# First two column tiles of the recurrent layer's input: turned by VectorE from PSUM and carried by DMAs, in place of ScalarE staging and TensorE transposes

## The reference

```python
WIDTH = 1536          # 12 chunks of 128 channels
def recurrent_mixer(h, w_in, conv_w, conv_b, gate_w, gate_b, lam, w_out):
    u = jnp.einsum('bsd,dc->bsc', h, w_in)
    gate, xb = u[..., :WIDTH], u[..., WIDTH:]
    xb = causal_depthwise_conv(xb, conv_w, conv_b)      # 4 taps along the tokens
    y = rg_lru(xb, gate_w, gate_b, lam)
    return jnp.einsum('bsc,cd->bsd', y * jax.nn.silu(gate), w_out)
# rg_lru: per chunk of 128 channels g = sigmoid(u @ gate_w + gate_b), split in r and i,
#   log_a = -8 * r * softplus(-lam); h_t = a_t * h_(t-1) + sqrt(1 - a_t^2) * (i * u)_t
```

## Time and profile before

| what | value |
|---|---|
| median of three executions | 880.54 us |
| the profiled execution | 880.93 us |
| its span, first to last instruction | 879.2 us |
| TensorE (PE) busy | 870.7 us, 99% of the span |
| VectorE (DVE) busy | 594.1 us, 68% |
| ScalarE (ACT) busy | 453.8 us, 52% |
| GpSimd (POOL) busy | 238.1 us, 27% |
| mean granted TensorE clock | 0.998 |

### The profile page before, as it was taken

The page is one execution under the profiler, slowest core; times in us unless marked ns, Lnnn a source line. Parts: engine busy times, 40 slices in busy tenths (PEclk is TensorE's granted clock), DMA queues, the critical chain, the costliest instruction groups (busy, mean ns, idle before and its releaser), DMA issues.

```text
span 879.2 us, 10563 instructions
## 1 busy us (share of the span) xinstructions
PE 870.7 (99%) x4152; PEld 729.2 (83%) x4152; DVE 594.1 (68%) x692; ACT 453.8 (52%) x560; POOL 238.1 (27%) x393
## 2 busy tenths in 40 slices
PE   9999999999999999999999999999999999999997
PEld 6788888888888888888888888888999888888885
DVE  6757666467767756567666666546979866777774
ACT  6745444445445557436444445445887544444433
POOL 2544453003021100000144446000390004444560
PEclk9999999999999999999999999999999999999999
DMA  9976666455753544555666666546535348666631
GB/s 341 370 236 217 220 223 221 144 192 186 278 201 116 194 151 188 192 192 191 238 219 218 216 216 222 192 179 245 183 113 192 144 172 296 216 222 215 219 121 48
DMA packets 36673, 178.75 MB, mean 203 GB/s; under 512 B 8481, under 2 KB 9553, under 8 KB 17681
## 3 DMA queue, kind: packets, MB, share of 16 engines
q1 hardware_dynamic: 24368, 161.23, 50.7%
q0 software_dynamic: 11968, 16.59, 6.4%
q10 hardware_dynamic: 288, 0.27, 0.1%
HBM read 167.05 MB, written 1.05 MB: 191 GB/s over the span
## 4 chain that ended last, share of the span: by engine, by line
PE 94%; DVE 2%; ACT 2%; DMA 1%; SPq 1%; issue 0%; ACTq 0%; DVEq 0%
PE acc L1583 26%; PE acc L1585 26%; PE acc L1584 26%; PE acc L1780 2%; PE acc L1950 2%; PE acc L1951 2%; PE acc L1949 2%; DMA raw<-weights 1%; DVE w_lo L974 1%; PE aux L1934 1%; PE aux L1701 1%; PE acc L1782 1%; PE aux L1583 1%; PE aux L1585 1%; PE aux L1584 1%; ACT w_hi L534 0%
## 5 line engine op out<-in xcount | busy, mean ns | idle before, releaser
L974 DVE TENSOR_TENSOR w_lo<-raw,w_hi 128x2048 fp32r<-128x2048 f32 x147 | 337.3, 2301 | 123.2 <-ACT w_hi L534 123.1
L534 ACT ACTIVATE w_hi<-raw 128x2048 fp32r<-128x2048 f32 x145 | 276.5, 1915 | 59.2 <-DMA raw<-weights 58.9
L1583 PE MATMUL acc<-w_hi,xT 128*128 128x512 f32 x760 | 298.4, 393 | 0.6 <-DVE w_lo L974 0.6
L1585 PE MATMUL acc<-w_hi,xT 128*128 128x512 f32 x760 | 296.1, 390 | 0.0
L1584 PE MATMUL acc<-w_lo,xT 128*128 128x512 f32 x760 | 295.8, 389 | 0.0
L1583 PEld LDWEIGHTS acc<-w_hi,xT 128*128 128x128 f32 x760 | 142.7, 188 | 30.6 <-DVE w_lo L974 1.0
L1585 PEld LDWEIGHTS acc<-w_hi,xT 128*128 128x128 f32 x760 | 142.6, 188 | 29.9
L1584 PEld LDWEIGHTS acc<-w_lo,xT 128*128 128x128 f32 x760 | 142.8, 188 | 28.9
L457 POOL DMA_DIRECT2D hT_raw<-turned x192 | 109.6, 579 | 122.0 <-DVE turned L1134 120.3
L520 POOL DMA_DIRECT2D b_moved<-b_turned x112 | 63.5, 575 | 71.4 <-DVE b_turned L1487 69.7
L1583 PE MATMUL acc<-w_hi,hT_hi 128*128 128x512 f32 x176 | 68.6, 390 | 0.0
(11 more groups left out here) (231 smaller groups left out, 1013.2 us busy)
## 6 DMA issues: line engine op xcount, KB each, us to landing
raw<-weights SPq DMA_DIRECT2D x147, 1024.0 KB, 4.9
hT_raw<-turned POOLq DMA_DIRECT2D x160, 32.0 KB, 2.7
gain_pre<-gains POOLq DMA_DIRECT2D x5, 512.0 KB, 5.2
b_moved<-b_turned POOLq DMA_DIRECT2D x80, 32.0 KB, 2.4
raw<-weights SPq DMA_DIRECT2D x4, 512.0 KB, 8.2
gain_post<-gains POOLq DMA_DIRECT2D x3, 512.0 KB, 5.9
gate_w<-gate_w_in POOLq DMA_DIRECT2D x1, 1536.0 KB, 9.2
x_turned<-x_turned_in SPq DMA_DIRECT2D x4, 256.0 KB, 5.2
```

The source lines that it names most:

```text
L534: a.activation(w_hi[:, g % RING], raw[:, g % RING], ACT.Copy).then_inc(hi_done, 1)
L974: v.tensor_tensor(w_lo[:, slot], raw[:, slot], w_hi[:, slot].bitcast(F32), ALU.subtract)\
L1583: m.matmul(dst, hi[:, k, cols], w_hi[:, slot, w], start=first, stop=False)
L1585: return m.matmul(dst, lo[:, k, cols], w_hi[:, slot, w], start=False, stop=last)
```

## The change

The 16 transposes on TensorE and the four copies on ScalarE are taken out. VectorE turns each 128x512 part of the two column tiles straight from PSUM in 32x32 blocks (turn_columns). For each column tile j, 16 DMAs carry the blocks to their quarter of the partitions: eight on SyncE's queue, behind the loads of groups g0+7 (for j = 0) and g0+9 (for j = 1), and eight on GpSimd's queue. Both queues first wait for the turns of both token tiles. The convolution then reads SBUF, and conv_start(f) waits for both halves of the DMAs of its column tile. TensorE's pairs now wait for VectorE's turns instead of ScalarE's copies, and its gates for conv_rest as before under another semaphore.

```diff
+        a_turned = [at(f"a_turned{j}", [P, 4, T, QUADS, 32], F32, place) for j, place in enumerate((area + 63488, temp_at))]
+        a_moved = [at(f"a_moved{j}", [P, 4, T, QUADS, 32], F32, area + 36864 + 4096 * j) for j in range(2)]
+        def a_blocks(j, i, q):
+            return (a_moved[j][32 * q:32 * q + 32, :, :, i, :].rearrange("p c t b -> p (c t) b"),
+                    a_turned[j][32 * i:32 * i + 32, :, :, q, :].rearrange("p c t b -> p (c t) b"))
# SyncE, in the loop over the groups, behind the load of group g
+                if g - RING in (FIRST_GROUP["a_in"] + 1, FIRST_GROUP["a_in"] + 3):
+                    j = (g - RING - FIRST_GROUP["a_in"]) // 2
+                    for t in range(T):
+                        sp.wait_ge(acc_free_dve[t], ACC_ORDER[:FIRST_ACC["a_in"] + j + 1].count("V"))
+                    for i in range(QUADS // 2):
+                        for q in range(QUADS):
+                            dst, src = a_blocks(j, i, q)
+                            sp.dma_start(dst, src).then_inc(a_landed[j], 16)
# GpSimd, behind load_gains(4, None, 7)
+            for j in range(2):
+                for t in range(T):
+                    pool.wait_ge(acc_free_dve[t], ACC_ORDER[:FIRST_ACC["a_in"] + j + 1].count("V"))
+                for i in range(QUADS // 2, QUADS):
+                    for q in range(QUADS):
+                        dst, src = a_blocks(j, i, q)
+                        pool.dma_start(dst, src).then_inc(a_rest_landed[j], 16)
# ScalarE
                 if f < A_STRAIGHT:
-                    act.wait_ge(bank_full, f0 + f + 1)
+                    act.wait_ge(a_landed[f // 2], 8 * MOVES)
+                    act.wait_ge(a_rest_landed[f // 2], 8 * MOVES)
-            round_to(g0 + 4)
-            stage_columns(0, 0)
-            round_to(g0 + 5)
-            stage_columns(1, 0)
-            round_to(g0 + 6)
-            stage_columns(0, 1)
+            round_to(g0 + 7)
             conv_start(0)
             conv_start(1)
-            round_to(g0 + 7)
-            stage_columns(1, 1)
             round_to(g0 + 8)
             conv_start(2)
# VectorE
+            def turn_columns(j, t):
+                dve.wait_ge(acc_full[t], c0 + j + 1)
+                v.transpose(a_turned[j][:, :, t].rearrange("p c q b -> p c (q b)"),
+                            acc[:, t, j].rearrange("p (c n) -> p c n", c=4)).then_inc(acc_free_dve[t], 1)
+            turn_columns(0, 0)
+            turn_columns(1, 0)
+            low_to(g0 + 5)
+            turn_columns(0, 1)
             low_to(g0 + 6)
+            turn_columns(1, 1)
             conv_rest(0)
# TensorE: staged_transposes and both of its calls are gone
-            first_columns(3, "a_in", lambda half: staged_transposes(0) if half else None)
+            first_columns(3, "a_in")
-                    if (b, half) == (1, 0):
-                        staged_transposes(1)
```

More of the change, by code:

```diff
@@ L60 @@
 ACC_READERS = {"f1_in": "V" * 11, "f1_out": "V", "mix_in": "AVVVVVVVVAAAA", "na_out": "V", "mix_out": "V",
-               "f2_in": "V" * 11, "f2_out": "V", "a_in": "AA", "a_out": "V", "b_in": "V" * 12, "b_out": "V"}
+               "f2_in": "V" * 11, "f2_out": "V", "a_in": "VV", "a_out": "V", "b_in": "V" * 12, "b_out": "V"}
 ACC_ORDER = "".join(ACC_READERS.values())
@@ L69 @@
                ("yret", 4), ("merged", 4), ("t2", 4), ("t3", 4),
-               ("a_in", 4), ("t4", 4)]
+               ("t4", 4)]
 FIRST_FILL = {name: sum(n for _, n in FILL_COUNTS[:i]) for i, (name, _) in enumerate(FILL_COUNTS)}
@@ L232, in build @@
         gate_w = at("gate_w", [P, CH, 2, P], F32, area + 51200)
-        a_stage = [at("a_stage0", [P, T, 512], F32, area + 63488), at("a_stage1", [P, T, 512], F32, temp_at)]
+        a_turned = [at(f"a_turned{j}", [P, 4, T, QUADS, 32], F32, place) for j, place in enumerate((area + 63488, temp_at))]
+        a_moved = [at(f"a_moved{j}", [P, 4, T, QUADS, 32], F32, area + 36864 + 4096 * j) for j in range(2)]
         yg_0 = at("yg_0", [P, 4, 512], F32, temp_at)
@@ L322, in build @@
         gate_w_in_s = sem("gate_w_in_s")
+        a_landed = [sem(f"a_landed{j}") for j in range(2)]
+        a_rest_landed = [sem(f"a_rest_landed{j}") for j in range(2)]
+        x_convolved = sem("x_convolved")
         conv_head = sem("conv_head")
@@ L364, in pair_bank, with conv_source @@
             return acc[:, b % 4 // 2, b % 2]
+        def a_blocks(j, i, q):
+            return (a_moved[j][32 * q:32 * q + 32, :, :, i, :].rearrange("p c t b -> p (c t) b"),
+                    a_turned[j][32 * i:32 * i + 32, :, :, q, :].rearrange("p c t b -> p (c t) b"))
+        def conv_source(f, k):
+            if f >= A_STRAIGHT:
+                return pair_bank(f - A_STRAIGHT)[:, k * S:(k + 1) * S]
+            return a_moved[f // 2][:, 2 * (f % 2) + k].rearrange("p t i b -> p (t i b)")
         block = ctx.enter_context(nc.Block())
@@ L794, in _ @@
             norm(*NORMS[3])
-            g0, c0, f0 = FIRST_GROUP["a_in"], FIRST_ACC["a_in"], FIRST_FILL["a_in"]
+            g0, c0 = FIRST_GROUP["a_in"], FIRST_ACC["a_in"]
             def conv_start(f):
                 if f < A_STRAIGHT:
-                    act.wait_ge(bank_full, f0 + f + 1)
+                    act.wait_ge(a_landed[f // 2], 8 * MOVES)
+                    act.wait_ge(a_rest_landed[f // 2], 8 * MOVES)
                 else:
                     act.wait_ge(pair_full, f - A_STRAIGHT + 1)
-                source = aux[:, f % 2] if f < A_STRAIGHT else pair_bank(f - A_STRAIGHT)
                 for k in range(2):
                     ch = 2 * f + k
-                    a.activation(u[:, ch], source[:, k * S:(k + 1) * S], ACT.Identity,
+                    a.activation(u[:, ch], conv_source(f, k), ACT.Identity,
                                  bias=conv_ab[:, ch:ch + 1], scale=conv_a[:, ch, 3:4]).then_inc(conv_head, 1)
@@ L837, in root @@
                              bias=zero[:], scale=-1.0).then_inc(mult_ready, 1)
-            def stage_columns(c, t):
-                act.wait_ge(acc_full[t], c0 + c + 1)
-                act_frees(t, a.activation(a_stage[c][:, t], acc[:, t, c], ACT.Copy))
             def gate_tanh(p):
@@ L1374, in conv_rest @@
                         ch = 2 * f + k
-                        i = v.scalar_tensor_tensor(u[:, ch, lag:], source[:, k * S:(k + 1) * S - lag],
+                        i = v.scalar_tensor_tensor(u[:, ch, lag:], conv_source(f, k)[:, 0:S - lag],
                                                    conv_a[:, ch, 3 - lag:4 - lag], u[:, ch, lag:], ALU.mult, ALU.add)
@@ L1378, in conv_rest @@
                             step(i)
-                i.then_inc(bank_free if f < A_STRAIGHT else pair_taken, 1)
+                i.then_inc(x_convolved if f < A_STRAIGHT else pair_taken, 1)
+            def turn_columns(j, t):
+                dve.wait_ge(acc_full[t], c0 + j + 1)
+                v.transpose(a_turned[j][:, :, t].rearrange("p c q b -> p c (q b)"),
+                            acc[:, t, j].rearrange("p (c n) -> p c n", c=4)).then_inc(acc_free_dve[t], 1)
             def with_rate(m):
@@ L1727, in out_stage, with first_columns @@
                         after_first()
-            def first_columns(n, st, in_last=None):
+            def first_columns(n, st):
                 run = norm_transposes(n)
@@ L1741, in first_columns @@
                 column_tile(g0, 0, 1, operand(1))
-                column_tile(g0 + 2, 1, 1, in_last)
+                column_tile(g0 + 2, 1, 1)
             def swiglu(which, n):
@@ L1903, in _ @@
             swiglu("f2", 2)
[L1906 to L1921, removed]
+            g0, c0 = FIRST_GROUP["a_in"], FIRST_ACC["a_in"]
+            n_dve = ACC_ORDER[:c0].count("V")
             def lru_gates(ch):
                 if ch < 8:
-                    pe.wait_ge(bank_free, f0 + ch // 2 + 1)
+                    pe.wait_ge(x_convolved, ch // 2 + 1)
                 else:
@@ L1942, in pair_product @@
                     if b < 4:
-                        pe.wait_ge(acc_free_act[b // 2], n_act + 1 + b % 2)
+                        pe.wait_ge(acc_free_dve[b // 2], n_dve + 1 + b % 2)
                     else:
```

## The result

The changed kernel takes 888.9 us (median, 888.3 to 890.2) against 880.5 (880.3 to 880.8): ratio 1.0097, 95% interval 1.0084 to 1.0110. It is 8.4 us slower, 6.2 above the forecast and 2.6 above the top of the range. The direction was right, the size was not. The profiled run took 890.2 us with a span of 888.1. It is the longest of the four, 1.3 above their median, where the profiled run before lies 0.4 above its own. So the two traces together show a loss near 9.3, and the medians 8.4.

A forecast was written before the change was run, and what follows sets the result against it. TensorE, busy 99% of the span, was taken to bound the kernel; the late second lot gives back the 1.5 us won and loses 2.2 more: 880.54 + 2.2 = 882.7 us, range 880.9 to 886.3.

The forecast's parts named there:

- Where the bound lies: TensorE's chain, 623.80 to 629.42 us, where its own work and ScalarE's path meet; shifting gates 2 and 3 reaches the end.
- The transposes and the turns: Removing TensorE's two blocks of eight transposes wins at most 1.75 us; VectorE's turns from PSUM take 0.71 each.
- The first lot: DMAs of blocks for chunks 0 to 3 land about 619.0; gates 0 and 1 start at 623.0, 1.5 us earlier.
- The second lot: DMAs of blocks for chunks 4 to 7, behind two loads, land at 626.5 (bounds 623.7 and 630.6); ScalarE starts 2.2 later.
- The way from ScalarE to TensorE: From ScalarE's start behind the second lot to TensorE's gates 2 and 3: 5.14 us, as before.
- A: Rival: loads do not hold up the small transfers; second lot lands 623.7 to 625.4, kernel 880.0 to 881.6 us; chance 0.25.
- D: Rival: second lot there before about 622.5, so the transposes' 1.75 us stay won; 878.6 us; chance 0.04.
- C: Rival: SyncE takes 0.98 us per DMA of small pieces; second lot lands at 630.6, kernel 886.8 us; chance 0.10.
- B: Rival: TensorE's clock falls in the new 3.9 us idle time, costing 1.9 us; 884.6 us; chance 0.18.
- VectorE does not add to it: VectorE's convolutions and low parts end at 633.4, before TensorE wants them at 636.4; priced at nothing.

The follow-up runs named there:

- experiment 7: Changed kernel, SyncE issuing lot 1 before g0+7's load and lot 2 before g0+8's and g0+9's, ScalarE's gates 0 and 1 before lot 2, VectorE's low parts reordered: 884.8 us.
- experiment 11: Changed kernel with only column tile 0 turned, its blocks before g0+7's load; tile 1 copied and transposed as before; ScalarE's gates and a low part earlier: 881.2 us.
- experiment 1: Changed kernel plus 26 unused matmuls on TensorE before gates 2 and 3: 891.3 us.
- experiment 2: Changed kernel plus 13 unused matmuls on TensorE before gates 2 and 3: 886.9 us.
- experiment 5: Changed kernel with ScalarE taking the gates of chunks 0 to 3 before the convolution start that waits for the second lot: 884.9 us.
- experiment 3: Changed kernel with SyncE issuing both lots ahead of the loads of g0+8 and g0+9: 885.2 us.
- experiment 4: Changed kernel with each DMA carrying one 1 KB run per partition instead of eight of 128 bytes, values landing in wrong places: 889.1 us.
- experiment 6: Changed kernel with the edits of experiment 3 and experiment 5 together: 885.6 us.
- experiment 8: As experiment 7, but GpSimd starts its input gates only after VectorE has convolved all four tiles: 888.0 us.

## Why the prediction was right or wrong

**Where the bound lies: right.** The chain at the earlier trace rows was the place, and the shift went through to the end: 9.4 us at gates 4 and 5, 9.3 at the end.

**The transposes and the turns: right.** Without its wait of 2.31 TensorE would have started gates 0 and 1 at 622.57, or 622.94 in the clock of before; 623.0 was forecast. The turns from PSUM took 0.72 (0.71 assumed) and ended at the forecast times.

**The first lot: 2.4 us too early.** 619.0 was forecast; the last block was issued at 616.89 and landed 4.1 later, at 621.4 in the clock of before. I had priced its landing with rows that have no load beside them, while the load of g0+7 had gone out 0.8 us ahead of the eight. That load explains 1.0 to 1.1 of the 2.4: with the lot ahead of it, it is there at relative 18.1 and 18.0 (experiments 7 and 11), not 19.1. What holds the rest was not tried. Gates 0 and 1 waited 2.31 us for it, which took the transposes' gain away before the second lot came into play.

**The second lot: the step that failed.** "So I put the whole lot at 625.4 + 1.1 = 626.5." It was there at 631.2 (630.84 + 0.37), above even my upper bound of 630.6; the three other traces with SyncE's order unchanged (experiments 1, 2 and 5) have it at 630.2 to 630.9. The term assumed that two loads and sixteen blocks pass as one load and a few blocks did in the earlier trace rows. Here the engines that move the data were full: the share is 0.95 over 15 us in the changed kernel. A window of its SyncE (the columns are the window, its length, the granted clock, the share and GB/s):

```profile
610.00:625.00 15.00, 1.00 0.95 298
```

The second load took 10.9 us to land, not 7.2, and every block behind it waited, from either queue. It is the amount ahead that I had wrong, more than the share: from 490 to 494 us of the trace before, around the 3.9 us that I had taken from the earlier trace rows, the share was 1.00 as well. Experiment 3 takes the loads out of the way and has the lot at 624.8; experiment 4 leaves 0.7 to 1.8 us at most for pieces and issue time. The Trainium skill, in DMA: Bandwidth & Descriptors, section "Anatomy of one DMA — SWDGE (gpsimd) path", gives a fixed part of about 2.0 us for one DMA, nearly constant. Here GpSimd's last block took 7.3, so behind two loads the measurement decides.

**The way from ScalarE to TensorE: right.** 5.14 was forecast, 636.14 - 630.87 = 5.27 was measured. Experiment 5 shows that half of the loss hangs on this order: 4.0 us come back by it alone.

**Rivals A and D** fell with the lot. **C** named the late lot (630.6, 886.8 us) by a cause that experiment 4 refutes as the main one, SyncE's issue; the first eight went out at 0.66 each, where C wanted 0.98. **B**, the clock, came true: 1.9 was its price, 2.0 to 2.4 the measurement (experiment 2). The error was to hold B and C for exclusive. A later lot lengthens the pause in which the clock fell, so the two prices add up; both together are 886.8 + 1.9 = 888.7, and 888.9 was measured. That the two agree so closely is partly luck, since the landing alone varies by 1 us from run to run. The rule that I had weighed for B, by the Trainium skill (TensorE: Matmul & The Clock Gate, "Part 1: The HAM clock gate"), was that the throttled level is the default and activity releases it. The trace agrees: 6.4 us without work, then 0.50 of the clock.

**"VectorE does not add to it": right by luck.** It held because TensorE was late anyway. As soon as the transfers are out of the way (experiments 3, 6, 7), the convolution of the blocks is the next bound. The turned copies lie in SBUF, where the transposed ones lay in PSUM, and I had taken for them, which have no operation of GpSimd's beside them, only its DMA issues. Beside GpSimd's input gates the six operations take 5.33 us, else 2.70. The Trainium skill states this in SBUF — State Buffer, section "Who interferes with whom": an instruction of VectorE with two inputs in SBUF contends with one of GpSimd that reads SBUF, and one with a single such input (outside VectorE's two-port modes) does not. Experiments 7 and 8 agree, and so does the trace of before, where I could have seen it: GpSimd's operation takes 0.73, and 2.67 when VectorE's low part (two inputs in SBUF) runs beside it. These are its rows, from the timelines of GpSimd and VectorE of the kernel before:

```profile
644.28 0.73 POOL L505 TENSOR_TENSOR ri<-ri,u 128x256 f32<-128x256 f32 x1
645.09 2.67 POOL L506 TENSOR_TENSOR ri<-ri,u 128x256 f32<-128x256 f32 x1
...
644.74 2.42 DVE L974 TENSOR_TENSOR w_lo<-raw,w_hi 128x2048 fp32r<-128x2048 f32 x1
```

**What stays open.** No version with two turned tiles came below 884.8 us. Experiments 3, 5 and 7 reach 884.8 to 885.2 by different roads, and their last 4 us are spread over waits of 1 to 2 us for VectorE and ScalarE. The contention was shown to be one of these; its whole price was not isolated, since the one way to remove it moved GpSimd's own work. No kernel tried beats the one before.

## What to carry to other kernels

- Before small transfers are put on a path, look at what their queue and the engines that move the data are doing in that window. Behind two loads of 1 MB, at a share of 0.95, SyncE's blocks of 32 KB took 3.9 to 8.6 us to land, not 2. Issuing them ahead of the loads brought the lot six us forward; making them of fewer pieces brought 1.8 at most.
- Rivals that feed each other need a joint price: a longer wait and the fall of the clock belong in one sum.
- An operand that moves from PSUM to SBUF changes who contends with whom. Count an engine's inputs in SBUF and ask what GpSimd reads at that time; and place an instruction that waits for a new transfer behind those that don't need it.

## What the runs showed of the hardware

- A load of 1 MB behind another and eight blocks: 10.9 us to land (7.2 was the longest that I had read ahead). SyncE's issue of a block behind two such loads: 1.15 us from start to start on the mean, 1.99 at most, against 0.66; with one piece per partition 0.66 on the mean there too.
- A block of 128-byte pieces makes 272 packets from SyncE and 32 from GpSimd: 4352 more in the one queue and 512 in the other, for 16 DMAs each. With one piece per partition (experiment 4) it is 48 from SyncE and 32 from GpSimd. Lines of the pages, packets, MB and share of time, first of the kernel before and then of the changed one:

```profile
q1 hardware_dynamic: 24368, 161.23, 50.7%
q0 software_dynamic: 11968, 16.59, 6.4%
```

```profile
q1 hardware_dynamic: 28720, 161.76, 50.8%
q0 software_dynamic: 12480, 17.12, 6.7%
```

- A turn of 128x512 from PSUM takes 0.72 us, as from SBUF.
- VectorE and GpSimd, both reading operands in SBUF, take turns: short operations alternate (0.89 each instead of 0.44 on VectorE), and a GpSimd operation of 0.74 that starts beside a low part of 2.3 lasts until shortly after that ends (2.7 to 2.8).
- TensorE's clock: after pauses of 6.41, 2.21 and 2.00 us (the changed kernel, experiments 5 and 4) it had fallen to 1.2 GHz, after pauses of 2.31 and 2.02 (the changed kernel, experiment 7) it had not. The length of a pause alone did not decide.
